# A hybrid decoder step on one core: four rows are spread over the partitions by transfers on GpSimd's queue, beside seven edits at the seams between stages

## What is computed

```python
def trunk_layer(x, c, ...):
    sh1, sc1, gt1, sh2, sc2, gt2 = split(silu(c) @ w_ada + b_ada, 6)
    h = rms_norm(x, g_mix) * (1 + sc1) + sh1
    x = x + gt1 * mixer_block(h, ...)          # two attention branches, gates, w_out
    h = rms_norm(x, g_ffn) * (1 + sc2) + sh2
    return x + gt2 * hier_moe(h, ...)

def hier_moe(h, ...):
    g_star = argmax(softmax(h @ w_rg + b_rg))            # one group of 4
    top_l, top_i = top_k(in_group_logits, 2)             # two experts of its 8
    combine = p_g * softmax(top_l)                       # two weights for a token
    # for each of the 32 experts, on the tokens routed to it:
    #   y = (silu(x @ w_eg[e]) * (x @ w_eu[e])) @ w_ed[e]
    # and every token sums its two experts' y by combine
```

## Time and profile before

| | before |
|---|---|
| median of 3 runs | 1081.83 us (1081.15 to 1085.96) |
| the profiled execution, its own time | 1082.4 us |
| its span, from first to last instruction | 1080.6 us |
| mean granted clock of TensorE | 0.971 of full speed |
| TensorE busy | 966.0 us (89%) |
| VectorE, ScalarE, GpSimd busy | 385.9, 294.1, 71.5 us |
| DMA | 318.82 MB, mean 295 GB/s |

### The profile page before, as it was taken

The page is one execution under the profiler, slowest core; times in us unless marked ns, Lnnn a source line. Parts: engine busy times, 40 slices in busy tenths (PEclk is TensorE's granted clock), DMA queues, the critical chain, the costliest instruction groups (busy, mean ns, idle before and its releaser), DMA issues.

```text
span 1080.6 us, 21869 instructions
## 1 busy us (share of the span) xinstructions
PE 966.0 (89%) x7598; PEld 605.2 (56%) x7599; DVE 385.9 (36%) x1083; ACT 294.1 (27%) x681; POOL 71.5 (7%) x145
## 2 busy tenths in 40 slices
PE   4799999999999997889889999989999899788995
PEld 2467677467864444434456767755786444343443
DVE  2126823223262332223353583132327133222234
ACT  2325565410042111101144455551003211110112
POOL 1012000000100000000001110000010000000000
PEclk9889999999999999989999999999999899999998
DMA  9894322899375999999997333289941399999991
GB/s 374 307 418 171 117 79 95 341 421 411 120 312 213 421 422 422 420 390 410 422 419 237 120 115 118 69 300 421 420 178 40 148 411 422 422 421 419 397 396 44
DMA packets 65420, 318.82 MB, mean 295 GB/s; under 512 B 6050, under 2 KB 27874, under 8 KB 28226
## 3 DMA queue, kind: packets, MB, share of 16 engines
q1 hardware_dynamic: 63408, 314.86, 72.8%
q10 hardware_dynamic: 1810, 2.51, 0.7%
q0 software_dynamic: 128, 0.40, 0.1%
HBM read 315.24 MB, written 2.51 MB: 294 GB/s over the span
## 4 chain that ended last, share of the span: by engine, by line
PE 67%; DMA 13%; DVE 8%; ACT 6%; issue 4%; SPq 1%; POOLq 0%; ACTq 0%; POOL 0%; DVEq 0%; PEldq 0%
PE ps L598 19%; DMA ring<-wstream 13%; PE ps L1098 9%; PE ps L680 7%; PE ps L1075 5%; PE ps L1088 4%; PE ps L1107 4%; PE ps L636 3%; PE ps L1010 3%; PE ps L1078 2%; ACT work L1297 2%; PE ps L746 1%; DVE work L1475 1%; DVE top L1474 1%; ACT L1297 1%
## 5 line engine op out<-in xcount | busy, mean ns | idle before, releaser
L1098 PE MATMUL ps<-ring,h 128*32 128x512 f32 x896 | 113.9, 627 | 25.2 <-DMA ring<-wstream 21.2
L598 PE MATMUL ps<-h,ring 128*128 128x288 f32 x512 | 131.2, 409 | 1.0 <-ACT work L1215 0.9
L598 PE MATMUL ps<-work,ring 128*128 128x288 f32 x512 | 128.7, 409 | 2.4 <-DVE work L1566 2.4
L598 PEld LDWEIGHTS ps<-work,ring 128*128 128x128 f32 x512 | 95.9, 190 | 28.5 <-issue 3.3
L598 PEld LDWEIGHTS ps<-h,ring 128*128 128x128 f32 x512 | 94.9, 190 | 29.1 <-issue 4.4
L680 PE MATMUL ps<-h,ring 128*128 128x288 f32 x416 | 105.0, 413 | 4.3 <-ACT h L1225 2.4
L1361 ACT ACTIVATE mraw<-ps 128x512 f32<-128x512 f32 x64 | 38.2, 597 | 244.8 <-PE ps L1098 244.4
L680 PEld LDWEIGHTS ps<-h,ring 128*128 128x128 f32 x416 | 79.5, 193 | 28.9 <-issue 7.2
L1107 PEld LDWEIGHTS ps<-fold,mraw 128*128 128x128 f32 x512 | 62.0, 191 | 52.0 <-ACT mraw L1361 43.0
L1719 DVE COPY yb<-ps 128x256 f32<-128x256 f32 x64 | 27.2, 425 | 170.0 <-PE ps L1088 170.0
L1107 PE MATMUL ps<-fold,mraw 128*128 128x32 f32 x512 | 68.9, 278 | 20.9 <-PE ps L1088 18.2
(11 more groups left out here) (252 smaller groups left out, 1025.6 us busy)
## 6 DMA issues: line engine op xcount, KB each, us to landing
ring<-wstream SPq DMA_DIRECT2D x272, 1024.0 KB, 15.4
work<-wstream SPq DMA_DIRECT2D x16, 1024.0 KB, 19.0
work<-pages SPq DMA_DIRECT2D x32, 192.0 KB, 3.2
work<-pages SPq DMA_DIRECT2D x32, 128.0 KB, 2.2
x<-x_in SPq DMA_DIRECT2D x1, 1152.0 KB, 5.6
out_y<-h ACTq DMA_DIRECT2D x2, 576.0 KB, 2.8
cs<-consts SPq DMA_DIRECT2D x1, 1026.0 KB, 9.0
out_vp<-work ACTq DMA_DIRECT2D x2, 256.0 KB, 3.2
```

The costliest lines, as they stand in the source:

```text
L598: last = mm(out, w[:, (k0 + k) * stride:(k0 + k) * stride + 128], rhs(k), start=(k == 0), stop=(k == n - 1))
L1098: last = mm(pgu[32 * c:32 * c + 32, :], xs[:, k, :], ws[k // 4][:, c * 512:(c + 1) * 512], start=(k < 4), stop=(k >= 4), skip_group_check= ...
```

## The change

1. `spread_row` and VectorE's four copies go. GpSimd issues four transfers from SBUF to SBUF. Each reads one row of `rows4` (one partition, 1152 bytes) 128 times and writes it to the 128 partitions of `drow`. VectorE, and GpSimd itself, wait for all four (`rows_spread`) ahead of their expert loops.
2. GpSimd's waits for the gathers' copies stand inside its loop, just ahead of the first staging.
3. `up` waits for its second piece only between its two halves, no longer ahead of both.
4. The sums of squares go to four groups of 32 partitions, 72 tokens each (`QT`), so that mean, root and reciprocal work on 128 x 72 values. Four matmuls with a repeated column of the identity then spread them to 128 x 288 in `pgut`, where VectorE reads them.
5. The samples' part of the sum goes ahead of chunk 4 of the prompt's (`SAMPLES_AT`).
6. ScalarE runs one root on an unused value after its expert loop, so that the table of the root is loaded there.
7. At the start the constants come in two transfers: 384 columns ahead of the weights and 1668 behind the ninth piece. ScalarE's first shift waits for less, and TensorE's first projection for the samples instead.
8. `y` is stored by four transfers of two chunks each.

```diff
@@ SyncE, the start
-            sp.dma_start(cs[:, :], consts).then_inc(start_in, 16)
+            sp.dma_start(cs[:, 0:C_SUM], consts[:, 0:C_SUM]).then_inc(start_in, 16)
...
+                if i == KD + 1:
+                    sp.dma_start(cs[:, C_SUM:C_END], consts[:, C_SUM:C_END]).then_inc(consts_in, 16)
@@ GpSimd, ahead of the experts and in their loop
+                banks.wait_drained(g, l, "rows")
+                for i in range(4):
+                    g.dma_start(drow[:, i, :].unsqueeze(1), bc(rows4[i:i + 1, :].unsqueeze(1), [1, 128, T])).then_inc(rows_spread, 16)
                 look_ahead(slice(0, 1))
-                far_kept.wait(g, l)
-                for k in range(FAR, KD):
-                    for hf in range(2):
-                        banks.wait_drained(g, l, f"x{k}.{hf}")
+                g.wait_ge(rows_spread, (l + 1) * 16 * 4)
                 hold(g, seen)
                 with g.Fori(0, N_EXP) as e:
                     with g.Fori(0, g.snap(n_blocks, min_val=1, max_val=MAXBLK)) as b:
                         n = g.snap(seen, min_val=0, max_val=200)
                         at = within(g.snap(first_slot, min_val=0, max_val=SLOTS) + b * BLK)
+                        far_kept.wait(g, l)
+                        for k in range(FAR, KD):
+                            banks.wait_drained(g, l, f"x{k}.1")
                         g.wait_ge(gu_done, n + 1)
@@ TensorE, the gathers
-                            if hf and k0 == 0 and c % 2:
-                                spread_row(2 * tb + c // 2)
@@ TensorE, an expert's first matmuls
-                def up(ws):
+                def up(e, rounds=0):
...
                         c = k % 4
-                        last = mm(pgu[32 * c:32 * c + 32, :], xs[:, k, :], ws[k // 4][:, c * 512:(c + 1) * 512],
+                        if c == 0:
+                            w = expert_weight(e, k // 4, rounds)
+                        last = mm(pgu[32 * c:32 * c + 32, :], xs[:, k, :], w[:, c * 512:(c + 1) * 512],
@@ TensorE, the sums of squares
+                def token_sums(m, samples):
+
+                    for c in range(4):
+                        at, to = c * QT, min((c + 1) * QT, NP)
...
+                        last = mm(pgu[32 * c:32 * c + 32, at - c * QT:to - c * QT], ones[:, 0:32], squared[:, m, at:to],
+                                  start=(m == 0 and not samples), stop=(m == KD - 1), skip_group_check=True)
...
+                keep_warm(1)
                 if l + 1 < DEPTH:
-                    keep_warm(5)
+                    norm1.wait(pe, l + 1, 2)
+                else:
+                    pe.wait_ge(final, 2)
+                for c in range(4):
+                    last = mm(pgut[:, c * QT:(c + 1) * QT], bc(ident[:, 32 * c:32 * c + 1], [128, 128]), rms[:, 0:QT], start=True, stop=True)
+                last.then_inc(spread_roots, 1)
@@ ScalarE, the start, the end of the experts and the end
-                    norm1.wait(a, l, 4)
+                    norm1.wait(a, l, 2)
+                    mods.wait(a, l, 1)
...
+                act(stat[:, 2, 0:1], stat[:, 2, 0:1], ACT.Sqrt).then_inc(sqrt_set, 1)
+                a.wait_ge(sqrt_set, l + 1)
...
-            for k in range(0, KD, 4):
-                a.wait_ge(final, 2 + k + 4)
-                a.dma_start(y_out[:, k:k + 4, :], h[:, k:k + 4, :]).then_inc(y_stored, 16)
+            for k in range(0, KD, 2):
+                a.wait_ge(final, 2 + k + 2)
+                a.dma_start(y_out[:, k:k + 2, :], h[:, k:k + 2, :]).then_inc(y_stored, 16)
@@ VectorE, ahead of the experts
-                for i in range(4):
-                    take(f"bc{i}", drow[:, i, :], banks.ap(l, f"bc{i}")[:, 0:T])
-                for i in range(4):
-                    banks.wait_drained(d, l, f"bc{i}")
-
+
+                d.wait_ge(rows_spread, (l + 1) * 16 * 4)
```

102 lines of the change are left out of this document (62 added, 40 removed).

## The result

The changed kernel takes **1093.31 us** (median of 7 runs, 1089.73 to 1095.71), the kernel before 1081.83 (1078.67 to 1085.96). The ratio is 1.010 with a 95% interval of 1.0073 to 1.0127, so between 7.9 and 13.7 us more. The profiled execution took 1092.74 us with a span of 1091.0; its mean granted TensorE clock is 0.959, that of before 0.971.

A forecast was written before the change was run, and what follows sets the result against it. TensorE's chain and the weight stream, whose restart after each gather sets the stage's end, were taken as the bound. Seams -11.5 and rows' transfers +21.9 give +10.4 on 1082.4, 1092.8; by the runs' median 1092 us, range 1070 to 1120.

The forecast's parts named there:

- What bounds the kernel: Both layers' experts: the weight stream restarts after the gathers, and moving that restart moves the stage's end by as much.
- The start: Kernel start: fewer constants ahead of `mod0`'s pieces, -2.0 us, and ScalarE's first shift not waiting for VectorE, -0.6.
- The join: Between the layers: shorter sums, root and reciprocal let ScalarE's last shift end at 559.4 instead of 562.5, -3.1 us.
- The end: Kernel end: the same steps as between the layers, -3.1 us, and a last transfer half as large, -0.8.
- `up` in halves: Experts: where the second weight piece is late, half of `up` is done before it lands, -0.95 us twice, -1.9.
- The transfers' rate: Four row transfers, 590 KB from one partition each: a sixteenth of the full rate, landing some 25 us after issue.
- Who waits: VectorE and, dearer, GpSimd before its first staging; second `up` 4.0 us after landing: +10.4 us layer 0, +10.7 layer 1.
- The stream: Weights during the reads: four pieces issued 3.3 us earlier, the next three late for slots: +11.2 and +10.7 us.
- The sum: Whole kernel: -11.5 us from the seams and +21.9 from the rows' transfers make +10.4.
- Hidden: Rival: one source partition yields the full rate, rows land after some 6 us, unwaited for; 1063 us, chance 0.13.
- The break-even: Rows' landing time at which the kernel, with the seams' gain, equals the one before: about 20 us, 34 GB/s.

The follow-up runs named there:

- the joined kernels: The changed kernel and follow-up kernels that keep its edits other than the rows' transfers; 11 with late pages took 291.0 to 294.9 us from join to layer 1's rows.

## Why the prediction was right, and where it was not

**What bounds the kernel.** Right in its use: each us by which the rows came sooner or later moved the end by 2 us. Halving the bytes brought 10.9 us a layer and 21.4 in all.

**The start, -2.6.** The last piece of `mod0` starts TensorE at 28.92 instead of 31.19 (-2.3; -2.0 forecast), and TensorE's first projection starts 2.8 sooner. The rows of layer 0 came 3.4 sooner; over the joined kernels that place scatters between 318.7 and 322.3, so the last 0.6 is no finding.

**The join, -3.1.** Its own steps are right (12.3 us, 12.4 forecast). The step that failed is the tacit one that a stage which starts 3.1 us sooner ends 3.1 us sooner. It was taken for TensorE's chain alone; the pages, timed by the stream of weights, were left out of it. They show in no wait of the trace of before, but their landings do: the last came 2.6 us ahead of its use (583.6 and 586.17), less than the 3.1 to be gained, and they became the bound. In its place: +0.9 in the trace, 4.0 off.

**The end, -3.9.** 14.4 us instead of 17.6, -3.2. The stores of 288 KB land in 2.1 us, and the spreading matmuls ran at the lower clock, 1.47 us at 1083.44 where the same ones took 1.11 in the join.

**`up` in halves, -1.9.** 2.2 us by the run without it, as far as its interval can tell.

**The transfers' rate.** The number is right, 24.9 and 24.8 us where 25 were forecast, and 27.0 GB/s by the slope where 26.3 were taken. The reason held too. The prediction took a group of eight partitions as what has a sixteenth of the rate, whoever asks; the runs show four neighbours held to 26 GB/s together, and two of three such groups sharing one way. That the change reads four partitions of one group made the order of the transfers irrelevant. The prediction had no word on that order, nor on how many engines a transfer is dealt to. Had the change read four neighbours of distant groups in each transfer, as the run with 18.5 us did, the same reasoning would have been over 6 us off. The decisive choice, the source and not the queue, held in both runs made for it.

**Who waits.** GpSimd's staging, then `up` 3.4 us later (4.0 forecast). Relative to the rows `up` came 9.9 us later in both layers; 10.4 and 10.7 were forecast. (The first of these has a slip: 325.3 + 25 + 4.0 is 354.3, not 354.1, so +10.5 and, further on, +11.4 in place of +11.2.)

**The stream.** The step "the extra pieces and two ring pieces are issued 3.3 us earlier than now" failed. They were issued at 331.49, but SyncE's two issues took 11.58 us instead of 0.80, and the pieces flowed only once the reads were over, from 345 on (the window from 344 to 346 moved 203 GB/s in the mean, the next one 406). The prediction had the engines "mostly free" during the reads; the windows show them held at 28 GB/s. The stream thus restarted 23.5 us after the rows (345.0 - 321.5) instead of 14.2 (338.14 + 0.9 - 324.88): +9.3. It then had its four pieces to load until about 357, and the first slots of the next came free at about 355.5 (5.24 us after `up`), so it never paused. The forecast's +11.2, from slots that come late to an idle stream, was the right size by another way. From the rows to the end of the experts layer 0 takes 10.1 us more than in the run in which TensorE spreads, and so does layer 1: 20.2 in the traces, 23.9 by the medians, 21.9 forecast.

**The sum.** +10.4 was forecast and the spans differ by 10.4, but not because each term was right: the join gave 4.0 less than forecast and the end 0.7 less; the experts of layer 1 were 2.8 shorter, those of layer 0 1.2 and the start 0.8. The experts' part lies within their scatter. A prediction that is right in total can be wrong by 4 us in a term.

**The rivals.** *Hidden* was given 1063: the three runs in which the rows hold up nobody and the pages are late have 1065.2 to 1067.3. The 2 to 4 us in between fit the join's gain that the pages took. The break-even at about 20 us stands between the run with one source per transfer (22.5 us, 1085.4) and the one with two rows (14.0 us, 1071.9).

## What to carry to other kernels

A copy within SBUF is priced by how many groups of partitions it reads at a time, before its bytes or its queue: spreading a row costs 1 us for each 27 KB written if one partition or its neighbours are read, and here it cost the kernel nothing once the row stood on eight partitions at a step of four. TensorE writes it there with a stationary of 32 equal columns. While a slow transfer held all DMA engines, register loads and the issues of another queue were late as well. When a seam is shortened, look for the transfer that is timed by another chain and lands next; moving its issue is often a change of one number.

## What the runs showed of the hardware

- Reads of one partition 128 times gave 27 to 30 GB/s; one transfer of four neighbours 26, of four partitions at a step of four some 103 (both by their packets), 128 partitions 263 over a stretch with the issues; the queue that issued made 0.7 us of 25.
- A transfer with four source partitions was carried by four engines, one with a single source repeated 128 times by all 16; so four of the first kind ran side by side (55 GB/s through two groups), and four of the second one after the other.
- While the slow reads ran, the DMA share was 0.97 and 1.05 in the two windows shown, at 28 and 30 GB/s. The share says how long engines are held, not what they move.
- In that time a register load from SBUF took 7.7 us instead of 0.28, and 6.3 from a partition that was not read; two issues of SyncE took 11.6 us instead of 0.80.
- Putting the sources of those four transfers on four distant partitions changed their landing only from 24.9 to 22.5 us.
- TensorE's clock fell to its lower level in a stand of 12.6 us and in and behind one of 3.6 us, and what ran behind it took up to 1.9 times as long (`up` 3.64 us for 1.92).
- GpSimd's fourth issue in layer 1 came 4.6 and 15.4 us late in the two runs with four sources per transfer, 0.4 us behind the last landing of the first three; why not in layer 0 is open.
